# Attention value products as three fp32r products of split operands, issued ahead of the gate units

## What is computed

```python
def gqa(q, k, v):
    ...
    s = jnp.einsum('bnkgd,bmkd->bkgnm', qg, k).astype(jnp.float32) * (d ** -0.5)
    p = jax.nn.softmax(s, axis=-1).astype(v.dtype)
    o = jnp.einsum('bkgnm,bmkd->bnkgd', p, v)

def diff_attn(q, k, v, lam, lam_init, subln_g):
    ...
    p = jax.nn.softmax(s, axis=-1)
    a = (p[:, :, 0] - lam * p[:, :, 1]).astype(v.dtype)
    o = jnp.einsum('bhnm,bmhe->bnhe', a, v)
```

## Time and profile before

| | |
|---|---|
| median of 3 runs | 2883.78 us (2883.55 to 2885.29) |
| span of the profiled execution | 2883.7 us |
| busy over the span: TensorE, VectorE, ScalarE | 2857.6, 1963.7, 1329.7 us |
| mean granted clock of TensorE | 0.999 |
| attention stage, first gate unit to first unit of the next phase | about 1608 to 1893 us |

### The profile page before, as it was taken

One profiled execution on the slowest core, in us unless ns is written; L12 is line 12 of the kernel. 1 busy time (PEld: TensorE's weight loads), 2 busy tenths in 40 slices (PEclk: granted clock), 3 DMA queues, 4 the chain that ended last, 5 costly groups with the idle time before them and its releaser, 6 DMA issues.

```text
span 2883.7 us, 34704 instructions
## 1 busy us (share of the span) xinstructions
PE 2857.6 (99%) x13679; PEld 2362.6 (82%) x13679; DVE 1963.7 (68%) x2525; ACT 1329.7 (46%) x1651; POOL 23.6 (1%) x47
## 2 busy tenths in 40 slices
PE   9999999999999999999999999999999999999999
PEld 8888788888888887788888777788878888888887
DVE  6876699999877668866647755567665555655444
ACT  5545554444444447532334555554454444444333
POOL 2000000000000000000000000000000000000000
PEclk9999999999999999999999999999999999999999
DMA  7545577777878877456656534358757777776664
GB/s 250 145 122 163 179 255 253 251 249 253 256 249 270 269 258 246 151 158 190 178 144 185 155 110 121 111 161 264 227 169 238 225 226 225 222 228 201 189 192 152
DMA packets 299953, 583.23 MB, mean 202 GB/s; under 512 B 18393, under 2 KB 18801, under 8 KB 299152
## 3 DMA queue, kind: packets, MB, share of 16 engines
q1 hardware_dynamic: 296896, 572.01, 63.8%
q0 software_dynamic: 2320, 7.96, 0.9%
q10 hardware_dynamic: 576, 1.05, 0.1%
HBM read 578.85 MB, written 2.10 MB: 201 GB/s over the span
## 4 chain that ended last, share of the span: by engine, by line
PE 94%; DVE 3%; ACT 1%; issue 1%; DMA 0%; SPq 0%; ACTq 0%; DVEq 0%
PE psum L560 22%; PE psum L563 22%; PE psum L562 22%; PE psum L629 3%; PE psum L627 3%; PE psum L628 3%; PE psum L2899 2%; PE psum L2901 2%; PE psum L2900 2%; PE psum L508 2%; PE psum L510 1%; PE psum L511 1%; PE psum L2917 1%; PE psum L2927 1%; PE psum L588 1%; PE psum L2952 1%
## 5 line engine op out<-in xcount | busy, mean ns | idle before, releaser
L692 DVE TENSOR_TENSOR w_lo<-w_raw,w_hi 128x1024 fp32r<-128x1024 f32 x720 | 877.7, 1223 | 581.3 <-ACT w_hi L686 577.5
L686 ACT ACTIVATE w_hi<-w_raw 128x1024 fp32r<-128x1024 f32 x720 | 762.7, 1060 | 1036.5 <-PE psum L563 1025.2
L560 PE MATMUL psum<-w_hi,x_split 128*128 128x512 f32 x1912 | 751.0, 393 | 1.2 <-DVE region_b L2260 1.0
L563 PE MATMUL psum<-w_hi,x_split 128*128 128x512 f32 x1912 | 745.5, 390 | 0.0
L562 PE MATMUL psum<-w_lo,x_split 128*128 128x512 f32 x1912 | 745.1, 390 | 0.0
L563 PEld LDWEIGHTS psum<-w_hi,x_split 128*128 128x128 f32 x1912 | 359.4, 188 | 75.3
L560 PEld LDWEIGHTS psum<-w_hi,x_split 128*128 128x128 f32 x1912 | 359.7, 188 | 75.0 <-issue 2.1
L562 PEld LDWEIGHTS psum<-w_lo,x_split 128*128 128x128 f32 x1912 | 359.8, 188 | 73.0
L560 PE MATMUL psum<-w_hi,hidden_split 128*128 128x512 f32 x704 | 274.9, 391 | 0.0
L563 PE MATMUL psum<-w_hi,hidden_split 128*128 128x512 f32 x704 | 274.0, 389 | 0.0
L562 PE MATMUL psum<-w_lo,hidden_split 128*128 128x512 f32 x704 | 273.9, 389 | 0.0
(11 more groups left out here) (373 smaller groups left out, 3543.0 us busy)
## 6 DMA issues: line engine op xcount, KB each, us to landing
w_raw<-in_w_in SPq DMA_DIRECT2D x216, 512.0 KB, 3.7
w_raw<-in_w_ada SPq DMA_DIRECT2D x192, 512.0 KB, 4.8
w_raw<-in_w_ffn_up SPq DMA_DIRECT2D x176, 512.0 KB, 4.5
w_raw<-in_w_ffn_down SPq DMA_DIRECT2D x88, 512.0 KB, 5.6
w_raw<-in_w_ff_gate SPq DMA_DIRECT2D x88, 512.0 KB, 4.1
w_raw<-in_w_ff_up SPq DMA_DIRECT2D x88, 512.0 KB, 3.8
w_raw<-in_w_ff_down SPq DMA_DIRECT2D x88, 512.0 KB, 4.2
w_raw<-in_w_out SPq DMA_DIRECT2D x64, 512.0 KB, 4.8
```

Source lines behind the costliest of these rows:

```text
L560: nc.tensor.matmul(to, x_hi[:, tokens], hi, start=u == 0 and t == 0, stop=False, skip_group_check=True)
L563: mm = nc.tensor.matmul(to, x_lo[:, tokens], hi, start=False, stop=end and t == 1, skip_group_check=True)
L686: nc.scalar.activation(w_hi[:, b.slot(n)], raw[:, b.raw_slot(k)], ACT.Copy).then_inc(w_rounded, 1)
L692: nc.vector.tensor_tensor(w_lo[:, slot], raw[:, b.raw_slot(k)], r(w_hi[:, slot]), ALU.subtract).then_inc(w_split, 1)
```

## The change

The value product is made like the large ones. The values of a head (or of the four "a" heads that share them) are split once: `v_high` on ScalarE copies a tile of 128 x 512 to a buffer `VH`, `v_low` on VectorE writes the remainder over the values. The transposed probabilities are split as they leave bank 6: ScalarE copies to `PTS[:, 0]`, and `turned_low` on VectorE subtracts, out of bank 6, to `PTS[:, 1]`. `PTS` has one buffer per head where `PTT` had two, in the same space, so ScalarE's copy of a head's first round now waits for the value products of the head before. These are 12 fp32r products of 256 columns, and they stand ahead of the round's gate units. Four semaphores of the query and key norms are merged into two (`head_sq` with `head_sum`, `head_std`), with their counts moved on; the queues keep their order there.

```diff
             WDT_SPLIT = freed("dt_split", [P, 2, KT, 32], F32R)
         with nc.sbuf_tensor("pad_s", [P, 22400], F32):
             SEL = freed("selector", [P, 32], F32R)
+        with nc.sbuf_tensor("pad_k", [P, 8192], F32):
+            KVR = freed("kv_split", [P, 24, 2 * L], F32R)
+        with nc.sbuf_tensor("pad_t", [P, 20480], F32):
+            PTS = freed("pt_split", [P, 2, 4, L], F32R)
         BF = sb("region_b", [P, NB])
 
         with nc.sbuf_tensor("pad_e", [P, NF * L], F32):
             PSP = freed("p_split", [P, 2, 2, L], F32R)
+            VH = freed("v_hi", [P, 2, 2 * L], F32R)
         EV = sb("evac", [P, 2, NF, L])
         EVF = EV.rearrange("p a f n -> p (a f n)")
...
                     exps(rd + 1)
                 for n in gate_units(rd - 1):
                     gate_hi(n)
+                if rd % 2 == 0 and v_new(rd // 2):
+                    v_high(rd // 2)
                 act.wait_ge(S("p_turn"), rd + 1)
-                if rd >= 4:
-                    act.wait_ge(S("pv_done"), rd // 2 - 1)
-                nc.scalar.activation(PTT[:, (rd // 2) % 2, :, qb * P:(qb + 1) * P],
+                if rd >= 2:
+                    act.wait_ge(S("pv_done"), rd // 2)
+                nc.scalar.activation(PTS[:, 0, :, qb * P:(qb + 1) * P],
                                      PS[:, 6, :].rearrange("p (c q) -> p c q", c=4),
-                                     ACT.Copy).then_inc(S("pt_ready"), 1)
+                                     ACT.Copy).then_inc(S("pt_hi"), 1)
                 if rd == O_FIRST:
...
+            def v_low(hd):
+                dve.wait_ge(S("v_hi"), v_count(hd))
+                v = v_tile(hd)
+                nc.vector.tensor_tensor(KVR[:, v], KV[:, v], r(VH[:, v_buffer(hd)]), ALU.subtract
+                                        ).then_inc(S("v_split"), 1)
+
+            def turned_low(rd):
+                dve.wait_ge(S("pt_hi"), rd + 1)
+                tokens = slice(rd % 2 * P, rd % 2 * P + P)
+                nc.vector.tensor_tensor(PTS[:, 1, :, tokens], PS[:, 6, :].rearrange("p (c q) -> p c q", c=4),
+                                        r(PTS[:, 0, :, tokens]), ALU.subtract).then_inc(S("pt_ready"), 1)
...
                     probabilities(rd)
                 for n in gate_units(rd - 1):
                     gate_lo(n)
+                if rd % 2 == 0 and v_new(rd // 2):
+                    v_low(rd // 2)
+                turned_low(rd)
                 if rd % 2 == 1 and rd >= 3:
                     output(rd // 2 - 1)
                 if rd == O_FIRST:
...
 
             def values(hd):
-                kind, h = HEADS[hd]
-                j = 4 + h // 4 if kind == "a" else 16 + h
                 pe.wait_ge(S("pt_ready"), 2 * hd + 2)
+                pe.wait_ge(S("v_split"), v_count(hd))
                 if hd >= 1:
                     pe.wait_ge(S("o_ready"), hd)
                 for c in range(4):
-                    mm = nc.tensor.matmul(PS[:, 7, 0:L], KV[:, j, c * P:c * P + P], PTT[:, hd % 2, c],
-                                          start=c == 0, stop=c == 3, skip_group_check=True)
+                    keys = slice(c * P, c * P + P)
+                    v_hi, v_lo = VH[:, v_buffer(hd), keys], KVR[:, v_tile(hd), keys]
+                    nc.tensor.matmul(PS[:, 7, 0:L], v_hi, PTS[:, 0, c], start=c == 0, stop=False, skip_group_check=True)
+                    nc.tensor.matmul(PS[:, 7, 0:L], v_lo, PTS[:, 0, c], start=False, stop=False, skip_group_check=True)
+                    mm = nc.tensor.matmul(PS[:, 7, 0:L], v_hi, PTS[:, 1, c], start=False, stop=c == 3,
+                                          skip_group_check=True)
                 mm.then_inc(S("pv_done"), 1)
...
                     ins = nc.tensor.transpose(PS[:, 6, c * P:c * P + P],
                                               PR[:, JOBS[rd][0] % 4, c * P:c * P + P], ident)
                 ins.then_inc(S("p_turn"), 1)
+                if rd % 2 == 0 and rd >= 2:
+                    values(rd // 2 - 1)
                 for n in gate_units(rd):
                     gate_unit(n)
                     if n - 3 in PHASES["gates"].done:
                         pe.wait_ge(S("pt_ready"), rd + 1)
                     ada_turn(pe, PHASES["gates"], n)
-                if rd % 2 == 0 and rd >= 2:
-                    values(rd // 2 - 1)
 
             def sub_stat():
                 for i in range(8):

```

`v_high` and the two functions that tell which tile and count belong to a head:

```diff
+        def v_tile(hd):
+            kind, h = HEADS[hd]
+            return 4 + h // 4 if kind == "a" else 16 + h
+
+        def v_buffer(hd):
+            return 1 if HEADS[hd][0] == "a" else 0
+
+        def v_new(hd):
+            kind, h = HEADS[hd]
+            return kind == "b" or h % 4 == 0
+
+        V_SPLITS = [hd for hd in range(len(HEADS)) if v_new(hd)]
+
+        def v_count(hd):
+            return max(V_SPLITS.index(x) + 1 for x in V_SPLITS if x <= hd and v_tile(x) == v_tile(hd))
+
         def o_split_to(q):
...
+                act.wait_ge(S("kv_freed_act"), KV_FREED_BY["act"])
+                act.wait_ge(S("kv_freed_dve"), KV_FREED_BY["dve"])
+                if hd >= 2:
+                    act.wait_ge(S("pv_done"), hd - 1)
+                nc.scalar.activation(VH[:, v_buffer(hd)], KV[:, v_tile(hd)], ACT.Copy).then_inc(S("v_hi"), 1)
 
```

More of the change, by code:

```diff
@@ L367, in build @@
         PR = bf(6144, 4, 512)
-        PTT = bf(20480, 2, 4, L)
         evA, evB = EV[:, 0], EV[:, 1]
@@ L597, in build @@
                 KV_FREED[_j, _k] = by, _n[by]
+        KV_FREED_BY = _n
         def kv_freed(eng, j, k):
@@ L1528, in kv_late @@
                         if n >= 2:
-                            act.wait_ge(S("k_sum"), n - 1)
-                        nc.scalar.activation(SQB[:, k % 2], KT_TOK[:, k], ACT.Square).then_inc(S("k_sq"), 1)
+                            act.wait_ge(S("head_sum"), n - 1)
+                        nc.scalar.activation(SQB[:, k % 2], KT_TOK[:, k], ACT.Square).then_inc(S("head_sq"), 1)
                 if u == 1:
-                    act.wait_ge(S("k_sum"), 4 * i + 4)
+                    act.wait_ge(S("head_sum"), 4 * i + 4)
                     root = KSS[:, :, 0:parts(kind)[0]]
                     nc.scalar.activation(root, root, ACT.Sqrt, bias=SM[:, 0:1],
-                                         scale=1.0 / parts(kind)[1]).then_inc(S("k_std"), 1)
+                                         scale=1.0 / parts(kind)[1]).then_inc(S("head_std"), 1)
                 if u == 6:
@@ L1554, in q_square @@
                     if g > 0:
-                        act.wait_ge(S("q_sum"), 2 * g - 1 + c)
+                        act.wait_ge(S("head_sum"), 12 + 2 * g - 1 + c)
                     else:
-                        act.wait_ge(S("k_sum"), 12)
-                    nc.scalar.activation(SQB[:, c], KT_TOK[:, 2 * (g % 2) + c], ACT.Square).then_inc(S("q_sq"), 1)
+                        act.wait_ge(S("head_sum"), 12)
+                    nc.scalar.activation(SQB[:, c], KT_TOK[:, 2 * (g % 2) + c], ACT.Square).then_inc(S("head_sq"), 1)
             def q_root(g):
-                act.wait_ge(S("q_sum"), 2 * g + 2)
+                act.wait_ge(S("head_sum"), 12 + 2 * g + 2)
                 kind = kind_of("q", g)
@@ L1564, in q_root @@
                 nc.scalar.activation(root, root, ACT.Sqrt, bias=SM[:, 0:1],
-                                     scale=1.0 / parts(kind)[1]).then_inc(S("q_std"), 1)
+                                     scale=1.0 / parts(kind)[1]).then_inc(S("head_std"), 1)
             def q_out(g):
@@ L1611, in exps, with v_high @@
                                          accum_out=SUMS[:, n:n + 1]).then_inc(S("exp_ready"), 1)
+            def v_high(hd):
+                act.wait_ge(S("kv_freed_act"), KV_FREED_BY["act"])
[3 more added lines that the diff above has]
+                nc.scalar.activation(VH[:, v_buffer(hd)], KV[:, v_tile(hd)], ACT.Copy).then_inc(S("v_hi"), 1)
             def o_hi(q):
@@ L2295, in kv_late @@
                     for k in range(4):
-                        dve.wait_ge(S("k_sq"), 4 * i + k + 1)
+                        dve.wait_ge(S("head_sq"), 4 * i + k + 1)
                         nc.vector.tensor_reduce(KSS[:, k, 0:nh], heads(SQB[:, k % 2], kind), AX.X,
-                                                ALU.add).then_inc(S("k_sum"), 1)
+                                                ALU.add).then_inc(S("head_sum"), 1)
                 if u == 1:
-                    dve.wait_ge(S("k_std"), i + 1)
+                    dve.wait_ge(S("head_std"), i + 1)
                     ch.mark(nc.vector.reciprocal(KSS[:, :, 0:nh], KSS[:, :, 0:nh]))
@@ L2334, in q_stage @@
                     for c in range(2):
-                        dve.wait_ge(S("q_sq"), 2 * g + c + 1)
+                        dve.wait_ge(S("head_sq"), 12 + 2 * g + c + 1)
                         nc.vector.tensor_reduce(QSS[:, c, 0:nh], heads(SQB[:, c], kind), AX.X,
-                                                ALU.add).then_inc(S("q_sum"), 1)
```

(3 more changed lines are left out.)

## The result

The changed kernel takes **2893.83 us** (median of 7 runs, 2892.52 to 2894.45) beside 2885.29 us for the kernel before, measured again on the same chip (7 runs, 2883.55 to 2887.3). The ratio is 1.0029, interval [1.002, 1.0038]: **slower by 8.5 us**, with the lower end of the interval just at the forecast's line of 0.2%. The forecast was 6.2 more, 2890.0, in a range of 2885.0 to 2896.5.

What follows compares the result with a forecast made beforehand. TensorE, busy 259.77 of 260 us in the attention stage, was taken as the bound; waits of 13.3 us minus 7.1 saved by the products gave +6.2, 2890.0 us. Own range 2886.8 to 2893.5, widened for rivals to 2885.0 to 2896.5.

Steps and rivals of the forecast that it cites:

- a stretch at 0.50 clock inside the stage: Sign in the attention stage's changed profile that would prove the prediction wrong through the clock falling there.
- Products: Attention value products on TensorE: 12 fp32r products at 0.12 us, 1.43 instead of 1.73 a head, 7.1 us saved.
- last head: Head 23's value product, stage end: needs bank 7 emptied by `output(22)`, delayed behind `turned_low(47)`; wait 1.9 us.
- rival B: Value products run at the array's pace, 0.108 us each: 3.5 us more saved, +2.7, 2886.5; chance 0.15.
- Even turns: Even-numbered of the 48 transpose turns (0 to 47): each loses 2.33 us of slack, 1.73 cover and 0.60 VectorE queue.
- Turn 34: Even transpose turn with slack 1.57 us before the change; predicted wait 0.8 us.
- Odd turns: Odd-numbered transposes: new "b" chain 5.4 us against 5.5 available; seven level turns 0.1 each, turn 33 waits 0.3.
- Rival D: The seven level odd turns tip by 0.4 us each: +9, 2893; chance 0.05.
- Turn 1: Second transposes, round 0, where nothing covers: `v_high` (0.5) goes before the copy, then `turned_low`; wait 1.6 us.
- Sum of waits: All TensorE waits predicted in the attention stage, from turn 1 to the last head's products: 13.3 us.
- rival A: Clock falls to 0.50 for 6.8 us after turn 42's 2.7 us stand, costing 3.4: +9.6, 2893.4; chance 0.24.
- The link from span to median: Whole kernel: profiled span 2883.7 us matched the median 2883.8 of three runs, so the sum was carried over unchanged.

Runs made afterwards that it cites:

- look: The change with VectorE's order turned round: next rounds' maxima and probabilities first, gate weights' low parts last, `output(23)` earlier, V's first high part earlier; 2880.35 us, ratio 0.9981.

## Why the prediction was right, and where it missed

The direction and the mechanism held; the size was 2.3 us short. By one of its own signs, a stretch at 0.50 clock inside the stage, the prediction was wrong in one step, the clock.

- **Products, -7.1.** Measured 7.1 to 7.2: 23 heads save 0.31 each (the starts of an even and the next odd turn without a wait come 0.30 to 0.32 closer), the last head 0.03. The spacing is 0.119 us; the array's pace of 0.108 (rival B) didn't come. The Trainium skill ("TensorE: Matmul & The Clock Gate", Wait — 56ns, not 53.3ns?) has products start every N / 2.4 ns plus 2.5 ns once the clock is at full, by which 256 columns would take an estimated 109 ns. The trace does not bear it out for this form.
- **Even turns, 2.33 us of slack lost.** Turn starts against those of before give: turn 6 1.0, turn 12 1.5, turn 24 0.9 (predicted 1.1 each); turn 16 1.8 (1.7); turn 46 0.7 (0.6); turn 42 2.3 (2.3). Turn 4 paid nothing (0.1).
- **Turn 34** paid 0.2, not 0.8, and turn 33 paid 0.7, not 0.3: the wait came one turn earlier. Together 0.9 for 1.1. The forecast put turn 33 down to the output split in the queue; the single buffer, to which the forecast gave no price, made that split 1.5 us late.
- **Odd turns.** Called level, at 0.1 each: turns 7, 13 and 25 paid 0.13 each, turn 19 0.1, turn 37 0.5. Rival D did not come. That they really are level is what the doubled subtraction showed: 0.6 us more in the queue, and 26 of 48 turns wait.
- **Turn 1** 1.7 (1.6; the copy of V takes 0.62 us, not 0.5), **last head** 2.0 (1.9).
- **Sum of waits**: about 14.3 where 13.3 were predicted. By turn starts: 6.7 at turn 47, plus 7.1 saved, less 1.5 of clock, plus 2.0 at the last head.
- **The clock, the step that failed.** The forecast left its fall at turn 42 out of the sum, as rival A with a chance of 0.24, deciding "from an idle time of 2.4 us on". It came: 1.5 us (1.4 by the run with idle products), half the 3.4 that A priced, since the slow stretch was 3.4 us long and not 6.8. And the bound was wrong: 1.94 us of idle time was enough with the fp32 products at the new place, 1.95 was not in the kernel without the subtraction. The idle time alone doesn't decide, so no such point can be read from one row. A's own 2893.4 lies close to the measured time by luck: its fall was priced at twice what it cost, and other terms made up for that.
- **The link from span to median.** The forecast took the profiled span of 2883.7 for the median, which the three runs then shown (2883.78) seemed to confirm. The kernel before measured 2885.3 and later 2885.7 in more runs, and the changed one took 2894.45 us in the run whose span is 2892.8. So some 1.6 us lie outside the span. Of the 3.8 us between 2890.0 and 2893.8, this link holds 1.6, the clock 1.5 and the waits 1.0, together 4.1; the 0.3 too much is what one profile may differ from a median.
- **The range.** The prices given with the sum lead to 2886.5 to 2892.9, where the forecast has 2886.8 to 2893.5 as its own range. The measured 2893.8 lies above either. It is inside the stated range only because that was widened for rival A, and A came.

-7.1 + 14.3 + 1.5 = 8.7, beside 8.5 measured. Before the savings the change thus costs 15.8. The profiled execution is the slowest of the seven runs of the changed kernel, and whether the clock fell at turn 42 in the others isn't shown, so the close agreement is in part luck. The span grew by 9.1; behind the stage the two profiles also differ in a fall of the clock (below), and the rest there wasn't taken apart.

The forecast read the order of VectorE's queue as given, and so did not see what the change could be worth. The 8.5 us were not the price of the products, but of a place without cover and of an order in which the next round's probabilities stand behind work that nobody waits for so soon.

## What to carry to other kernels

Where an engine is 99% busy, a move within its own queue can cost as much as new work: count for each wait what stands as cover between the release of the other engine's chain and the wait, before and after. When work is added to a second engine whose total has room, put what the bound engine waits for first in that queue, a round ahead if its inputs are there, and refills with slack last; then follow the tail, where the same order can hide an output behind a refill. A saving that doesn't show may be set free by such a reordering: here 8.5 us slower became 5.4 us faster with the same instructions.

## What the runs showed of the hardware

The granted clock can fall in one run and not in another after the same wait. Behind the stage, at the next norm, TensorE stands 1.67 us both in the kernel before and in the changed one; first before, then after (timelines):

```profile
2148.36 0.63 PE L906 MATMUL psum<-constants,region_b 128*128 128x128 f32 x4 [1.67 <-DVE evac L939]
```

```profile
2156.95 0.90 PE L911 MATMUL psum<-constants,region_b 128*128 128x128 f32 x4 [1.67 <-DVE evac L944]
...
2155.00:2158.60 3.60, 1.93 (x10) 1.53 (x9) 2.44 (x5) 1.75 (x3) 0.00 (x0) 0.80 0.56 209
```

The granted clock stays at 1.00 in the first and falls in the second (0.80 over the window; the transposes last 0.90 instead of 0.63), 1.7 us lost over a stretch of 3.4, from 2157.0 on. With the subtraction twice, the clock fell behind waits of 2.5, 2.4 and 3.0 us (turns 12, 16 and 42) and not behind one of 2.25 (turn 1). Likewise the fall behind `sub_stat` lasted 6.8 us in the kernel before and in the change, and 3.4 in `look`, which had another of 3.4 us far ahead of the stage, from 225 on. Differences of 2 us between two single profiles of this kernel can thus be the clock's alone, and only medians of many runs, or starts compared within one stretch, are to be read.
